# One step of a hybrid decoder layer: the low parts of 20 projection weight blocks move from POOL to DVE

## Time and profile before

| | us |
|---|---|
| median of 3 runs | 1093.77 |
| profiled execution, its own time | 1092.07 |
| its span, first to last instruction | 1090.2 |
| PE busy | 934.5 (86%) |
| DVE busy | 573.0 (53%) |
| ACT busy | 499.3 (46%) |
| POOL busy | 469.6 (43%) |

### The profile page before, as it was taken

One profiled execution on the slowest core, in us unless ns is written; L12 is line 12 of the kernel. 1 busy time (PEld: TensorE's weight loads), 2 busy tenths in 40 slices (PEclk: granted clock), 3 DMA queues, 4 the chain that ended last, 5 costly groups with the idle time before them and its releaser, 6 DMA issues. The chain is left out here.

```text
span 1090.2 us, 14288 instructions
## 1 busy us (share of the span) xinstructions
PE 934.5 (86%) x5034; PEld 780.6 (72%) x5034; DVE 573.0 (53%) x1018; ACT 499.3 (46%) x828; POOL 469.6 (43%) x343
## 2 busy tenths in 40 slices
PE   3899999999999999968999998269999999999800
PEld 2799887888788778845788875258888887777600
DVE  4413533353325332767651136777777777667347
ACT  4333344334432444254221121538888887777412
POOL 3202223222322322257231120075999985665575
PEclk9899999999999999977897799569999999999955
DMA  8022321322110211443354321869999999998785
GB/s 241 23 87 95 97 78 59 119 92 84 40 61 21 59 32 36 157 142 107 91 184 136 97 81 61 352 242 357 404 408 408 411 403 400 400 387 350 272 289 205
DMA packets 92410, 206.25 MB, mean 189 GB/s; under 512 B 12751, under 2 KB 54159, under 8 KB 84150
## 3 DMA queue, kind: packets, MB, share of 16 engines
q1 hardware_dynamic: 80718, 171.37, 43.7%
q0 software_dynamic: 7008, 17.18, 4.4%
q10 hardware_dynamic: 4616, 16.80, 3.8%
HBM read 171.19 MB, written 42.34 MB: 196 GB/s over the span
## 5 line engine op out<-in xcount | busy, mean ns | idle before, releaser
L958 PE MATMUL pj<-n_hi,w_hi 128*128 128x350 f32 (+1 forms) x576 | 200.9, 349 | 3.6 <-issue 2.1
L1786 POOL TENSOR_TENSOR e_lo<-e_raw,e_hid 128x2048 fp32r<-128x2048 f32 x32 | 167.1, 5223 | 73.7 <-ACT e_hid L1782 73.6
L958 PE MATMUL pj<-n_lo,w_hi 128*128 128x350 f32 (+1 forms) x576 | 189.2, 328 | 0.0
L958 PE MATMUL pj<-n_hi,w_lo 128*128 128x350 f32 (+1 forms) x576 | 188.4, 327 | 0.0
L1786 DVE TENSOR_TENSOR e_lo<-e_raw,e_hig 128x2048 fp32r<-128x2048 f32 x64 | 149.4, 2338 | 0.1
L658 POOL TENSOR_TENSOR w_lo<-w_raw,w_hi 128x1024 fp32r<-128x1024 f32 x24 | 57.1, 2381 | 202.5 <-ACT w_hi L739 202.5
L958 PEld LDWEIGHTS pj<-n_hi,w_hi 128*128 128x128 f32 x576 | 110.5, 192 | 33.1 <-issue 31.1
L1782 ACT ACTIVATE e_hig<-e_raw 128x2048 fp32r<-128x2048 f32 x64 | 122.8, 1920 | 23.6 <-DMA e_raw<-in_w_up 18.0
L1234 DVE CUSTOM_DVE_ANT_0 sc<-pj,strip 128x512 f32<-128x512 f32 (+5 forms) x120 | 61.5, 545 | 100.1 <-PE pj L1024 63.4
L958 PEld LDWEIGHTS pj<-n_lo,w_hi 128*128 128x128 f32 x576 | 110.7, 192 | 0.6
L958 PEld LDWEIGHTS pj<-n_hi,w_lo 128*128 128x128 f32 x576 | 110.4, 192 | 0.7 <-issue 0.6
(11 more groups left out here) (256 smaller groups left out, 1809.4 us busy)
## 6 DMA issues: line engine op xcount, KB each, us to landing
e_raw<-in_w_up SPq DMA_DIRECT2D x32, 1024.0 KB, 16.2
e_raw<-in_w_gate SPq DMA_DIRECT2D x32, 1024.0 KB, 18.7
e_raw<-in_w_down SPq DMA_DIRECT2D x32, 1024.0 KB, 19.2
expert_rows<-yo ACTq DMA_DIRECT2D x32, 512.0 KB, 7.9
w_raw<-in_w_in SPq DMA_DIRECT2D x24, 512.0 KB, 3.9
expert_rows<-logits SPq DMA_DIRECT2D x16, 512.0 KB, 5.2
k_page<-in_cache_k SPq DMA_DIRECT2D x16, 256.0 KB, 3.8
wo_raw<-in_w_out SPq DMA_DIRECT2D x8, 512.0 KB, 3.7
```

Of the source, the lines that this page charges most:

```text
L958: ins = pe.matmul(pj[g % 2][:, 0:tn], ws[w][:, P * k:P * (k + 1)], x[:, k, t0:t0 + tn], start=(m == 0), stop=(m == 23))
L1786: eng.tensor_tensor(e_lo[r][:, q, :], e_raw[r][:, q, :], e_hi(par, q).bitcast(F32), ALU.subtract).then_inc(s_lo[q], 1)
```

## The change

The low parts of blocks 4 to 23 of w_in are formed by DVE. POOL keeps those of blocks 0 to 3 and of the output weights. Even blocks are formed ahead of the scores of a tile (behind the combination and the convolution), odd ones behind the scores and ahead of the normalisation. A new semaphore `s_wld` counts them, and waits on the count of POOL's low parts are renumbered (4 instead of NB ahead of the output weights).

```diff
+        def dve_low_w(dve, n):
+            dve.wait_ge(s_whi, n + 1)
+            w = w_slot(n)
+            dve.tensor_tensor(w_lo[w][:], w_raw[w][:], w_hi[w][:].bitcast(F32), ALU.subtract).then_inc(s_wld, 1)
...
             for s in range(SLOTS):
-                for g in (chunk_b(s - 1),):
-                    for n in range(4, NB):
-                        if g is not None and FIRST[n] - 2 == g:
-                            pool_low_w(pool, n)
                 if (t := unit_at(s, 2)) is not None:
                     pool_root(pool, did, t)
                 if (h := head_at(s, 5)) is not None:
                     pool_cadd(pool, h)
-                for n in range(4, NB):
-                    if chunk_a(s) is not None and FIRST[n] - 2 == chunk_a(s):
-                        pool_low_w(pool, n)
...
             if m0 == 0:
-                pe.wait_ge(s_wlo, n + 1)
+                if n < 4:
+                    pe.wait_ge(s_wlo, n + 1)
+                else:
+                    pe.wait_ge(s_wld, n - 3)
...
                 if (h := head_at(s, 3)) is not None:
                     dve_conv(dve, did, h)
+                for n in range(4, NB):
+                    if chunk_b(s - 1) is not None and FIRST[n] - 2 == chunk_b(s - 1):
+                        dve_low_w(dve, n)
                 if s < NU:
                     dve_scores(dve, did, s)
                 g = chunk_a(s)
                 if g is not None and by_dve(g):
                     dve_evac(dve, g)
+                for n in range(4, NB):
+                    if g is not None and FIRST[n] - 2 == g:
+                        dve_low_w(dve, n)
                 if (t := unit_at(s, 2)) is not None:
                     dve_on(dve, t)
```

More of the change, by code:

```diff
@@ L298, in step_kernel @@
         s_wlo = sem("s_wlo")
+        s_wld = sem("s_wld")
         s_ch = sem("s_ch")
@@ L497, in load_wo @@
             else:
-                sp.wait_ge(s_wlo, NB + m - 2)
+                sp.wait_ge(s_wlo, 4 + m - 2)
             sp.dma_start(wo_raw[m % 3][:], I["w_out"][0][P * k:P * (k + 1)]).then_inc(s_wo[m % 3], 16)
@@ L922, in act_ad @@
                     else:
-                        act.wait_ge(s_wlo, NB + 8)
+                        act.wait_ge(s_wlo, 4 + 8)
                     act.activation(junk[0:M, :], h_sb[0:M, i % 2, :], ACT.Square, accum_out=hst[0:M, i % 2, 0:1]).then_inc(s_hsq, 1)
@@ L1039, in pe_mix @@
                 if i == 0:
-                    pe.wait_ge(s_wlo, NB + 4 * what + k + 1)
+                    pe.wait_ge(s_wlo, 4 + 4 * what + k + 1)
                 for a, (c, w) in enumerate(((hi, wh), (hi, wl), (lo, wh))):
```

## The result

| | before | after |
|---|---|---|
| median of 8 runs each, us | 1093.73 (1089.98 to 1097.62) | 1103.04 (1096.35 to 1106.68) |
| ratio | | 1.0083, 95% interval 1.0056 to 1.0109 |
| profiled execution, span, us | 1090.2 | 1094.5 |
| POOL busy, us | 469.6 | 418.9 |
| DVE busy, us | 573.0 | 578.2 |

Slower by 9.3 us, where 5.6 were forecast. In a later series the same kernel was slower by a ratio of 1.0105 (1.0080 to 1.0131). The profiled execution is the fastest of its eight, so its span understates the change; what it is good for is the slots. DVE is busy only 5.2 us longer, though it has 20 instructions of 1.22 us more, 24.5 us in all: about 19 us of stalls beside POOL are gone, which the prediction had at no more than 18.9.

The account below looks back on a forecast made before the run. PE was taken to bound the stage. Tile 4's 1.1 us plus tile 7's 4.5 us made 5.6 us, taking the profiled 1092.07 us to 1097.7 and the median to 1099.4 us; forecast's own range 1097.5 to 1102.

Parts of the forecast that it names:

- What bounds the stage, and what the removal gives: PE bounds the stage; removing 20 POOL subtractions of 2.39 us pays only through DVE stalls, felt by PE only at tile 4.
- Cost of the instruction: One low part on DVE takes 1.21 us and pushes the next instruction by 1.15 us; bounds 1.07 and 2.39 us.
- Odd blocks and tile 1: nothing: Ten low parts at tiles 2, 5, 8 and four even blocks at tile 1 cost PE nothing.
- Tile 4: Slots 4, 13, 22: scores start later, PE loses 0.37 us each, 1.1 us in all; bounds 0.9 to 4.8.
- Tile 7: Slots 7, 16, 25: scores wait for the low part, 1.49 us each, 4.5 us in all; bounds 3.6 to 8.1.
- The argument that the second map had no slack: At tile 7 PE's second piece already waits for DVE at its second map, so the whole 1.49 us falls on PE.
- the clock falls too: Rival, chance 0.20: PE's new waits lower the granted clock one to six times, adding 1.7 to 10 us, 1101 to 1109.
- Part is taken back: Rival, chance 0.15: PE's later waits for ACT, as behind tile 7, shrink and return 3.2 us, giving 1096.2 us.
- DVE's stalls were the price: Rival, chance 0.04: removing DVE's stalls beside POOL, at most 18.9 us, pays: some 13 us down, 1080 us.
- Nothing is won or lost: Rival, chance 0.05: the low parts land in time on which nobody waits, at tile 7 too; 1093.8 us.
- One example in the prediction: L1240 on DVE at tile 1, given as stalled beside POOL's subtraction: 2.27 us against a median of 0.17.
- The median: Profiled execution, 1092.07 us, lay 1.7 us below the runs' median 1093.77; so 1097.7 became a forecast median of 1099.4.

Follow-up runs that it names:

- behind: The changed kernel with the even blocks' low parts placed behind the scores, not ahead of them; 1089.49 us, ratio 0.9979 to the kernel before.
- no47: The changed kernel with the six low parts of tiles 4 and 7 back on POOL; 1092.13 us, ratio 0.9991 to the kernel before.
- cover: The changed kernel with 15, not 6, PE matmuls between the pieces of scores at tiles 4 and 7; 1085.17 us, ratio 0.9935 to the kernel before.
- twice7: The changed kernel with a second, unused subtraction ahead of the low part at tile 7; 1111.96 us, ratio 1.0179 to the kernel before.
- only7: The changed kernel with only tile 7's three low parts on DVE, the other 17 on POOL; 1098.09 us, ratio 1.0032 to the kernel before.
- only4: The changed kernel with only tile 4's three low parts on DVE, the other 17 on POOL; 1091.36 us, ratio 1.0005 to the kernel before.
- wait7: The kernel before, with DVE only waiting for the high part ahead of tile 7's scores; 1091.19 us, ratio 0.9989 to the kernel before.
- again: The changed kernel run once more, unaltered, for a second profile and more runs; 1100.44 us, ratio 1.0105 to the kernel before.
- before_cover: The kernel before, with 15, not 6, PE matmuls between the pieces of scores at tile 4; 1083.35 us, ratio 0.9925 to the kernel before.
- before_cover2: The kernel before with 15 matmuls between the pieces at tile 4, run a second time in another series; 1085.81 us, ratio 0.9946 to the kernel before.
- behind_cover: The changed kernel with even low parts behind the scores and 15 matmuls between the pieces at tile 4; 1083.90 us, ratio 0.9933 to the kernel before.

## Why the prediction was right in its direction and short in size

**What bounds the stage, and what the removal gives.** Right. PE is the bound, nobody waited for a low part, and the stalls that DVE had beside POOL's subtractions were worth only what the prediction said: at tile 4, and there alone. behind shows it: 2.4 us less in the slots.

**Cost of the instruction.** 1.21 us worked out on a line between two rows, 1.22 measured. It pushes the next one by 1.14 us (123.99 to 125.13), where 1.15 was taken.

**Odd blocks and tile 1: nothing.** Right, by no47.

**Tile 4.** 0.37 us each, 1.1 in sum; measured 0.30, 0.38 and 0.36, 1.04 in sum.

**Tile 7.** 1.49 us each, 4.5 in sum; measured 1.43 each, 4.3 in sum. The wait itself is 1.16 us, where about 1.3 was named, and the group behind it is 0.18 us longer, where some 0.2 was. The argument that the second map had no slack decided it: by the first map alone it would have been 1.3. It was confirmed from three sides, by the work taken away (behind), covered (cover) and doubled (twice7).

**The clock: this term of the sum was missing.** I took it at 0 and made it a rival with 0.20 ("the clock falls too", 1101 to 1109). The measured 1103.0 lies there, above the forecast's own end of 1102. The waits make 5.3 of the 9.3 us, and a mean granted clock that is 0.0032 lower makes 3.5. The weak step was to take nothing for the clock because the 0.96 us of tile 4 brought no fall: it was read from one execution. no47 and only7 show a fall behind the same wait, 0.90 us at slot 22.

The rival got the number, but not all of the mechanism. It had the falls behind the new, longer waits; behind the new waits of 1.16 us at tile 7 there is none in nine. Nor is it shown that 1.26 in place of 0.90 us at tile 4 makes a fall likelier: it came behind four of twelve waits of the one kind and two of twelve of the other, and only4's runs have no lower clock (0.9218, against 0.9196 for the kernel before in its series). What the runs do show is that the low clocks are more frequent in the kernels with waits at tile 7. A mean granted clock of 0.916 or less came in 16 of 76 runs of the kernel before, in 3 of 12 of both no47 and behind, in 1 and 0 of 12 of only4 and wait7, in 13 of 26 of the kernels with waits of 1.16 us (change, again, only7), in 6 of 6 of twice7, and in 1 of 37 of those whose waits are covered.

In the traces of the changed kernel (after and again) the six waits brought one fall each time, 1.7 us; the other 1.8 us of the 3.5 are not found in them. Behind slot 31 only7's trace has a granted clock of 0.55 over 480 to 520 us, where the profile before had 0.76, and from the first scores of slot 32 to those of slot 35 it takes 48.8 us, where the kernel before took 42.1. But before_cover's trace has the same 48.8 us, without a low part on DVE and without a wait at tiles 4 and 7, so such a fall does not need the change. The three parts of the change add up to less than the whole, too: the ratios of only4, only7 and no47 make 1.0028 together, the whole made 1.0083 and 1.0105, a gap about as large as the noise of these runs. Where the rest of the clock's share arises, and why more often here, stays open.

**The rivals.** "Part is taken back" falls: the wait for ACT at slot 8 is still 1.08 us. "DVE's stalls were the price" falls: only7, no47 and wait7 leave it nothing beyond tile 4. "Nothing is won or lost", the way the Trainium skill's Perfetto Trace Analysis (section "Optimizing Scalar/DVE Operations") would have it, describes the 14 low parts that stand where DVE has time; for the other six, place decided, and not the port. One example in the prediction is not what it is called: L1240 reads one tensor from SBUF, with a constant. The rows with two inputs are L1215 and L1217, stalled to 0.99 and 2.53 us.

**The median.** The sum was made on the profiled execution, and the 1.7 us by which it lay below the median of before were added at the end. That holds only if the profile of the changed kernel lies as far below its own median; after the change it is 6.7 us. A single profile of this kernel is a sample of the clock as much as of the code.

## What to carry to other kernels

Before work moves to an engine that has time, look at what stands behind the place where it goes: an engine that is half idle still has an instruction on which the bound engine waits, and an instruction that waits for a third engine holds that up too. Put such work behind the hand-over, not ahead of it, or give the bound engine something of its own to do across the wait; here that was worth more than the choice of engine. And where TensorE stands for a microsecond in a dense stretch, count the wait and what the clock may take behind it, over several executions.

## What the runs showed of the hardware that was not expected

A wait of about one microsecond on PE is followed by half the clock in some executions and not in others. Over the traces of all kernels, from slot 0 to slot 31:

| wait of PE | where | followed by a fall |
|---|---|---|
| 0.88 to 0.96 us | tile 4 (before, wait7, no47, only7) | 2 of 12 |
| 1.15 to 1.16 us | tile 7 (after, again, only7) | 0 of 9 |
| 1.26 us | tile 4 (after, again, only4, twice7) | 4 of 12 |
| 1.44 to 1.45 us | slot 31 (before, wait7, no47, only7, only4, behind, after, again, twice7) | 5 of 9 |
| 2.29 us | tile 7 (twice7) | 3 of 3 |
| covered by work | tile 4 and slot 31 (cover, before_cover, before_cover2, behind_cover) | 0 of 16 |

The longest ones cost 3.4 us of work at the first of them, the others about 1.7. The length is not all of it, by the row of tile 7; what sets the two kinds apart is open.

And of the spread of the times, over 14 us in the kernel before on one chip, most goes with the mean granted clock: over its 35 runs the two have a correlation of -0.94, and on the two other chips of -0.89 (26 runs) and -0.87 (15 runs).
